# Two transformer blocks on one core: the second feed-forward switches to the normalised x one chunk earlier, and eight modulation products move to the first feed-forward

## The reference, cut to what matters

```python
mod = silu(c) @ w_mod + b_mod                    # 2048 x 12288 weights
sh1, sc1, g1, sh2, sc2, g2 = split(mod, 6)
h = rmsnorm_2(x, mlp_norm_g) * (1.0 + sc2) + sh2
u = relu(h @ w_ff1)                              # second feed-forward
x = x + g2 * ((u * u) @ w_ff2)
```

## Time and profile before

| | |
|---|---|
| median of 3 runs | 2254.77 us (2253.86 to 2256.92) |
| the profiled execution | 2253.62 us |
| its span, first to last instruction | 2251.9 us |
| granted TensorE clock, mean | 0.999 |
| PE busy | 99% of the span |
| DVE busy | 82% |
| ACT busy | 52% |

### The profile page before, as it was taken

One profiled execution on the slowest core, in us unless ns is written; L12 is line 12 of the kernel. 1 busy time (PEld: TensorE's weight loads), 2 busy tenths in 40 slices (PEclk: granted clock), 3 DMA queues, 4 the chain that ended last, 5 costly groups with the idle time before them and its releaser, 6 DMA issues.

```text
span 2251.9 us, 34334 instructions
## 1 busy us (share of the span) xinstructions
PE 2229.9 (99%) x12802; PEld 1968.5 (87%) x12802; DVE 1846.7 (82%) x2873; ACT 1167.4 (52%) x1709; POOL 111.3 (5%) x211
## 2 busy tenths in 40 slices
PE   8999999999999999999999999999999999999998
PEld 7888889888888888888899899989988888888886
DVE  7887989899889898998889888998766666666666
ACT  6554665565445454454456668556644444434444
POOL 0000000000111111111010000000000000000000
PEclk9999999999999999999999999999999999999999
DMA  8556664578888888888875554556655555555553
GB/s 318 187 180 249 234 219 157 187 248 293 307 296 305 296 298 311 297 303 300 305 267 186 200 202 150 187 202 227 227 187 187 187 189 203 187 187 194 196 190 112
DMA packets 86883, 515.61 MB, mean 229 GB/s; under 512 B 9781, under 2 KB 10341, under 8 KB 37584
## 3 DMA queue, kind: packets, MB, share of 16 engines
q1 hardware_dynamic: 57600, 406.87, 49.9%
q0 software_dynamic: 28992, 106.43, 14.2%
q10 hardware_dynamic: 144, 0.26, 0.0%
HBM read 511.39 MB, written 2.14 MB: 228 GB/s over the span
## 4 chain that ended last, share of the span: by engine, by line
PE 89%; DVE 7%; ACT 2%; issue 1%; DMA 1%; SPq 0%; ACTq 0%; POOLq 0%; DVEq 0%
PE ps L588 22%; PE ps L602 11%; PE ps L912 8%; PE ps L911 8%; PE ps L910 8%; PE ps L662 8%; PE ps L667 4%; PE ps L658 3%; PE ps L659 3%; PE ps L660 3%; DVE wl L1665 3%; PE ps L694 1%; PE ps L696 1%; PE ps L695 1%; PE ps L739 1%; DVE modraw L1773 1%
## 5 line engine op out<-in xcount | busy, mean ns | idle before, releaser
L1665 DVE TENSOR_TENSOR wl<-raw,wh 128x1024 fp32r<-128x1024 f32 x762 | 928.8, 1221 | 293.9 <-ACT wh L1109 291.1
L1109 ACT ACTIVATE wh<-raw 128x1024 fp32r<-128x1024 f32 x766 | 805.4, 1056 | 637.0 <-PE ps L912 309.1
L588 PE MATMUL ps<-xs,wh 128*128 128x512 f32 x1744 | 417.1, 390 | 0.0
L588 PEld LDWEIGHTS ps<-xs,wh 128*128 128x128 f32 x1744 | 322.6, 188 | 63.8
L1773 DVE CUSTOM_DVE_ANT_0 modraw<-modraw,cb 128x1024 f32<-128x1024 f32 x192 | 233.6, 1219 | 18.8 <-DMA modraw<-in_wmod 18.4
L602 PE MATMUL ps<-xs,wl 128*128 128x256 f32 x1744 | 227.1, 283 | 0.0
L602 PEld LDWEIGHTS ps<-xs,wl 128*128 128x128 f32 x1744 | 221.9, 191 | 5.8
L662 PE MATMUL ps<-xs,wh 128*128 128x512 f32 x880 | 223.5, 396 | 0.0
L662 PEld LDWEIGHTS ps<-xs,wh 128*128 128x128 f32 x880 | 158.3, 189 | 29.7 <-issue 0.6
L588 PE MATMUL ps<-xc,wh 128*128 128x512 f32 x608 | 150.2, 389 | 0.0
L538 POOL DMA_DIRECT2D modraw<-in_wmod x172 | 90.8, 528 | 1041.4 <-DVE modp L1773 1037.9
(11 more groups left out here) (368 smaller groups left out, 3550.4 us busy)
## 6 DMA issues: line engine op xcount, KB each, us to landing
raw<-in_w SPq DMA_DIRECT2D x381, 1024.0 KB, 5.0
modraw<-in_wmod POOLq DMA_DIRECT2D x192, 512.0 KB, 4.8
x<-in_x SPq DMA_DIRECT2D x4, 512.0 KB, 8.9
raw<-in_w SPq DMA_DIRECT2D x4, 512.0 KB, 8.8
tbias<-rel_rows POOLq DMA_DIRECT2D x4, 512.0 KB, 6.5
cb<-c_silu POOLq DMA_DIRECT2D x1, 1024.0 KB, 4.8
g2row<-g_rows POOLq DMA_DIRECT2D x1, 1024.0 KB, 10.9
finrow<-in_fin POOLq DMA_DIRECT2D x1, 1024.0 KB, 5.1
```

The lines of the kernel that those rows point to most:

```text
L588: m = nc.tensor.matmul(PS[(b + bi) % 4][:, :], hi[:, t * P:(t + 1) * P], src[k].rearrange("p a t -> p (a t)"), start=opens and first and n ...
L1109: nc.scalar.activation(wh[:, h % HS, :], raw[:, u % RAW, (h % 2) * 1024:(h % 2 + 1) * 1024], ACT.Copy).then_inc(s_round, 1)
L1665: nc.vector.tensor_tensor(wl[:, h % HS, :], raw[:, (h // 2) % RAW, (h % 2) * 1024:(h % 2 + 1) * 1024], wh[:, h % HS, :].bitcast(F32), ALU. ...
```

## The change

The second chunk of the second feed-forward now reads `xs`, in paired units, like the chunks after it. For this the 16 blocks of `h` are made in units 2 to 7 (2, 3, 3, 2, 3, 3 of them) and PE waits for them ahead of the second chunk. `normed_lo` of a block comes in the same unit as its `normed`, no longer one unit later. The second chunk's results go the way of the later chunks (`units` with `relu2` on DVE). `LATE_MODS` is 10: no modulation product is left in the second feed-forward, `g2` is made in its second unit, and in four of the five down stages of the first feed-forward DVE makes 11 products and not 9 (two each at j = 2, 4 and 6, before only at j = 4). The products between take the places of earlier ones; none is added in all.

```diff
-        normed_in = lambda u: share(KB, u, 3, 14)
-        LATE_MODS = 18
+        normed_in = lambda u: share(KB, u, 2, CH)
+        LATE_MODS = 10
...
             ups(XD, name="mlp2", late_sums=N_MLP2, joined=True, paired=False)
-            ups(XD, joined=True, paired=False)
             pe.wait_ge(s_xs, XS["mlp2n"] + KB)
+            ups(XPAIR)
...
             def relu2(n):
 
                 y, u = c.n["y"], up[:, n % 2, :]
-                if n == CH:
-                    act.wait_ge(s_modu, NMOD)
                 add_bias("ffn2", n, u, ACT.Relu)
...
-            for n in range(2 * CH):
+                h_hi(hs2[0], n)
+
+            for n in range(CH):
                 step((lambda: root(N_MLP2)) if n == 2 else (lambda: relu2(n - 1)) if n > 2 else None,
-                     late=(lambda: (relu2(0), relu2(1))) if n == 2 else lambda: hi_normed(normed_in(n)))
+                     late=lambda: (relu2(0) if n == 2 else None, relu2(1) if n == 2 else None, hi_normed(normed_in(n))))
...
+            act.wait_ge(s_modu, NMOD)
+            ups2(hs2[1], lambda: relu2(CH - 1))
...
-                token_downs(chunk, lambda: gate_in(CH - 1), lambda: conv(CH - 1), lambda j: mods(1 + (j == 4)))
+                token_downs(chunk, lambda: gate_in(CH - 1), lambda: conv(CH - 1), lambda j: mods(1 + (j in (2, 4, 6))))
...
             def second_half(n):
-                if n < CH:
-                    mods(1)
-                if n == CH:
+                if n == 1:
                     dve.wait_ge(s_modu, NMOD)
                     mod_parts(5, 6, s_g2)
                 if n >= 3:
-                    h_lo(hs2[(n - 1) // CH], (n - 1) % CH)
-                normed_lo(normed_in(n - 1))
-
-            for n in range(2 * CH):
+                    h_lo(hs2[0], n - 1)
+                normed_lo(normed_in(n))
+
+            for n in range(CH):
                 half((lambda: relu_in(n - 1)) if n > 2 else None, after=lambda: first_half(n))
                 half((lambda: (relu_in(0), relu_in(1))) if n == 2 else None, after=lambda: second_half(n))
+            units(CH, relu2, first=lambda: relu_in(CH - 1), lo_first=lambda: h_lo(hs2[0], CH - 1), h_lo_of=lambda j: h_lo(hs2[1], j))
```

More of the change, by code:

```diff
@@ L1599, in relu2 @@
                 nc.scalar.activation(yf[:, y % 2, :], u, ACT.Square).then_inc(s_hy, 1)
-                h_hi(hs2[n // CH], n % CH)
-            for n in range(2 * CH):
+                h_hi(hs2[0], n)
+            for n in range(CH):
                 step((lambda: root(N_MLP2)) if n == 2 else (lambda: relu2(n - 1)) if n > 2 else None,
-                     late=(lambda: (relu2(0), relu2(1))) if n == 2 else lambda: hi_normed(normed_in(n)))
+                     late=lambda: (relu2(0) if n == 2 else None, relu2(1) if n == 2 else None, hi_normed(normed_in(n))))
             def x_by_token(i):
@@ L1625, in final @@
                     root_table()
+            act.wait_ge(s_modu, NMOD)
+            ups2(hs2[1], lambda: relu2(CH - 1))
             for n in range(NC2 - 2):
-                downs2((lambda: h_hi(hs2[(n + 1) % 2], CH - 1)) if n else lambda: relu2(2 * CH - 1), x_by_token if n == 0 else None)
+                downs2(lambda: h_hi(hs2[(n + 1) % 2], CH - 1), x_by_token if n == 0 else None)
                 ups2(hs2[n % 2])
@@ L2527, in _ @@
             for n in range(NC2 - 2):
-                downs2(n, (lambda: relu2(CH - 1)) if n else lambda: relu_in(2 * CH - 1),
+                downs2(n, lambda: relu2(CH - 1),
                        lo_first=lambda: h_lo(hs2[(n + 1) % 2], CH - 1))
```

## The result

The changed kernel takes 2267.89 us (median of 6 runs, 2267.28 to 2275.3) against 2253.69 of the kernel before (6 runs, 2253.3 to 2256.92) beside it: ratio 1.0066, 95% interval 1.0056 to 1.0075. Predicted were 2267 us. The profiled execution took 2267.29 us with a span of 2265.6, 13.7 more than before. The sum was right, but it is not built as predicted, as the rows show.

A forecast was written before the change was run, and what follows sets the result against it. PE was taken as the bound, 89% of the chain. Own time 2253.62 + 12.8 (four downs) + 0.1 (wait for h 2.0 less 1.9 gained) = 2266.5; the median lies 1.15 above, so 2267 us, range 2256 to 2283.

The forecast's parts named there:

- Eight products more in four down stages: First feed-forward: two tile buffers delay each down's last product 6.3 us, PE waits 3.2 us a down, 12.8 in all.
- the predicted slack of 3.1: Second unit after a down: a down's last product may come 3.1 us later before PE waits for its low weights.
- The landing: Product tiles in the downs: a load lands 6.05 us after its start, giving one product per 3.97 us.
- my own criterion: Four downs: the price begins where a tile's landing exceeds 5.2 us.
- What the waits show: DVE's waits for `modraw`: 30 us or more rather than 18.4, nearly all of the rise in the four downs.
- The new wait for h: Second feed-forward, ahead of the first paired unit: PE waits 2.0 us for all 16 blocks of h.
- PE's list: Second chunk of the second feed-forward: eight paired units of 5.54 us instead of 5.78 take 1.9 us less.
- `g2` earlier, products gone: nothing: Second feed-forward: eight products and 4 MB of loads leave, `g2` is written earlier, all costed at nothing.
- The tiles come in time: Rival, four downs: landing stays at or below 5.2 us and slack takes the rest; 2253.6 to 2255, chance 0.20.
- The DMA engines fill up: Rival, downs: DMA 0.93 busy, landing 7 us or more, PE waits 7 or more a down; over 2276, chance 0.20.
- ACT and DVE fall behind in units 2 to 7: Rival, second feed-forward: at 1 us more a unit PE waits 5 us for h; 2258 if tiles come in time, chance 0.04.
- The whole saving shows: Rival: no wait at 1577 and no lost down; 2252.9, 0.08% less; faster by over 0.2% has chance 0.01.

The follow-up runs named there:

- products only: Kernel before, with only the eight modulation products moved from the second feed-forward into four down stages of the first; 2266.16 us.
- DVE's work alone: Kernel before, with two low parts of weights made a second time in each of the four downs, no load added; 2254.58 us.
- one product more: Kernel before, with ten products in each of four downs (two each at j = 2 and 6), four left in the second feed-forward; 2256.31 us.
- doubles late: Changed kernel, with the doubled products of a down behind units 5, 6 and 7 instead of 2, 4 and 6; 2282.77 us.
- spread to the gates: Changed kernel, with the eight products moved one to each down and one to each gate stage of the first feed-forward; 2264.33 us.
- ten joined: The run switch only, with h spread over ten joined units and six paired ones following; second feed-forward 93.64 us against 93.88 before.
- nine joined: The run switch only, with h spread over nine joined units and seven paired ones following; second feed-forward 94.25 us against 93.88 before.
- doubles early: Changed kernel, with the doubled products of a down behind units 0, 2 and 4 instead of 2, 4 and 6; 2265.31 us.
- switch only: Changed kernel, with the eight products taken out of the downs and made in the per-layer gate projection; 2258.18 us.
- ten joined in place: Changed kernel, with the eight products left in the second feed-forward's first chunk and ten joined units; PE waits 5.66 us, total time not given.
- switch in place: Changed kernel, with the eight products left in the second feed-forward's first chunk, switch after eight units; 10.2 us more than before.

## Why the prediction was right, point by point

**Eight products more in four down stages.** The mechanism held: products alone 11.7 us, DVE's work alone nothing, and the loss follows the position of the doubles. The place and the pace held as well (3.88 us a product against 3.97, eight starts 31.0 against 31.8). The term was 12.8 us and the stretch lost 12.2, but the agreement is partly luck. (The recorded sum, 2266.5 + 1.15, comes to 2267.7 and not to 2267.) "PE waits 3.2 us a down" is wrong in size: the waits are 1.45 us behind the first down (0.56, 0.39, 0.50), 2.30 behind the second, 0.42 and 1.92 in and behind the third, 1.06 behind the fourth (0.68, 0.15, 0.23), 7.15 in all, and not 12.8. The sum had no term for the rest: 3.4 us of lower clock, 1.1 us of matmuls counted to their end ahead of a wait, 0.8 us untraced.

The slack is what held best. In the kernel before the last product of each down starts 43.3 us after the down's first matmul. In all ten downs of these runs that themselves ran no longer than before, and whose last product came more than 3.3 us later, PE's wait in the second unit behind the down is the lateness less 3.25 us, to 0.01. With the 0.16 us by which the profile shows a wait too short, that is the predicted slack of 3.1:

```
last product later by    wait of PE    run, down
3.94, 5.56               0.68, 2.30    changed kernel, fourth and second
5.61, 5.77               2.36, 2.52    products only, fourth and third
3.55                     0.29          one product more, second
4.14, 5.46               0.89, 2.21    doubles late, second and fourth
7.84, 8.19               4.59, 4.93    doubles late, first and third
4.53                     1.27          spread to the gates, fourth
```

What was mis-sized is the lateness: 6.3 us was predicted for every down, and in the changed kernel it was 2.5, 5.6, 5.9 and 3.9. The rival that the added loads hold up the weights' own isn't what happened: in the whole stretch no engine waits for `raw`.

**The landing.** I took 6.05 us, the mean of four medians. After the change the medians of the four downs are 5.7, 5.1, 4.9 and 5.2: all but the first at or below 5.2, where my own criterion says that the price begins. Last groups of the DMA view, changed kernel, second and fourth down:

```profile
modraw<-in_wmod POOLq DMA_DIRECT2D x9, 512.0 KB, 5.1
...
modraw<-in_wmod POOLq DMA_DIRECT2D x10, 512.0 KB, 5.2
```

So the median was the wrong number to sum with: turns in sequence take their mean, and the long landings weigh in it. From the pace itself, 2 x 3.88 - 1.89 = 5.9 us; the mean of the nine landings in that down is 6.05 us, with a median of 5.1. That it equals the 6.05 taken is luck: the means of the four downs were 6.2 to 6.7 before and are 5.6 to 6.05 after, so the landings became shorter. "If `modraw` lands in 5 us there and PE doesn't wait, the prediction is wrong": it landed in 5, and PE did wait. The GB/s of the four downs are 317, 301, 299 and 315, against 310, 318, 316 and 321 before, so the engines did not fill up. By the fit of the Trainium skill (DMA: Bandwidth & Descriptors, section Anatomy of one DMA), 3.2 us for 512 KB as an estimate, nothing would have been lost; the shortest landing in these four downs is 3.5 us and their means 5.6 us and more, so the trace doesn't agree with it beside the weights' loads. The loads of `modraw` that the kernel before issues at 1445.93 and 1463.17, with no other load in flight, land in 3.54 and 3.59 us, near it.

**What the waits show.** DVE's wait for `modraw` is over 30 us, as forecast. But not nearly all of the rise is in the downs: there it goes from 11.6 to 27.0 us, and from 18.2 to 42.9 in the whole stretch between the first and the fifth down. The lateness is carried on into the up and gate stages.

**The new wait for h.** Predicted 2.0 us, measured 2.94; the mechanism is the one walked out. Where the size is off shows in the timeline of DVE, changed kernel, the last unit ahead of the wait:

```profile
1586.49 0.42 DVE L1828 TENSOR_TENSOR tb<-ps,rstd 128x258 f32<-128x258 f32 x1
1586.83 1.22 DVE L1665 TENSOR_TENSOR wl<-raw,wh 128x1024 fp32r<-128x1024 f32 x1
1587.96 1.27 DVE L1865 SCALAR_TENSOR_TENSOR yn<-x,gmod,rstd 128x256 f32<-128x256 f32 x3
1589.35 1.23 DVE L1665 TENSOR_TENSOR wl<-raw,wh 128x1024 fp32r<-128x1024 f32 x1
1590.49 0.42 DVE L2197 TENSOR_TENSOR hs2a<-yf,hs2a 128x256 fp32r<-128x256 f32 x1
1590.82 1.27 DVE L1837 SCALAR_TENSOR_TENSOR xs<-yn,mod,xs 128x256 fp32r<-128x256 f32 x3
1592.01 0.42 DVE L1828 TENSOR_TENSOR tb<-ps,rstd 128x258 f32<-128x258 f32 x1
```

A unit with three blocks is 5.52 us, not 5.33: three `normed` with what follows take 1.39 rather than 1.20 us. Some four such units make 0.8 of the 0.94 us.

**PE's list.** Predicted -1.9 us. The second chunk took 1576.96 to 1623.04 before, 46.1 us, and 44.6 after: -1.5. A joined unit is 5.76 rather than 5.78 (0.2 us in eight), a paired one 5.56 rather than 5.54 (11.11 us for two in the timeline above, 0.1 in eight), and the first high run was 0.15 slower. From start to start the wait is 3.1 us (1588.93 + 0.12 to 1592.15), so 3.1 - 1.5 = +1.6 where the sum had +0.1. The unit's rate from two starts a third of a microsecond apart was too coarse for a difference of 4%.

**`g2` earlier, products gone: nothing.** Right. The write is issued at 1555.00, which is the predicted 1543 plus the 12.1 us by which this chunk starts later, and takes 11.5 us against 11.1 before, and no wait of PE follows it until the one for h, which DVE releases. The run "products only" shows the other half.

**The rivals.** "The tiles come in time" is refuted by the products alone. "The DMA engines fill up" is not what happened (299 to 317 GB/s). "ACT and DVE fall behind in units 2 to 7" didn't happen in the changed kernel, but it is what happens where the products stay (6.26 us a unit, 5.66 and 9.09 us of wait), so the move has a reason. "The whole saving shows" would have needed no wait for h: with ten joined units it is 0.24 us.

**Left open.** Why the clock stayed at 1.00 behind the 2.94 us wait in the changed kernel and fell behind the same wait in four other kernels. How much of the landing is due to weights in flight. A third buffer for `modraw`, which would test the turn directly, was not tried. No version was found that beats the kernel before: the two nearest, nine and ten joined, can't be told from it.

## What to carry to other kernels

A wait for a double-buffered load in the middle of an in-order queue is priced by the chain of turns (reuse to issue, issue to landing) against when each item is due, not by bytes or busy time: the same eleven loads a down cost 5, 12 or 19 us in the profiled executions by where the doubles stood. Take the pace from the mean landing, not the median, and don't put the extra items late in a stage. Where a saving on the path is 0.1% of the time, measure first what its preparation adds elsewhere: here it was 12 us for a saving of 1.5.

## What the runs showed of the hardware

**A short wait of PE is followed by a lower clock.** Behind waits of 1.86 us and more the granted clock was 0.50 for some 3 us after PE had resumed, behind those of 4.59, 5.66 and 9.09 us for 4 to 5, and those matmuls ran at half speed. In some it fell before the wait's end, in others up to 1.4 us after it. The means of windows of 3 to 5 us behind each wait (the longer ones, and those that start ahead of the fall, hold full clock too):

```
wait us            clock in the window behind it
0.89               1.00   doubles late
1.36               1.00   products only
1.51, 1.51         1.00   doubles early, nine joined
1.86               0.57   spread to the gates
1.92, 2.30         0.66, 0.55   changed kernel
2.21, 4.59, 4.93   0.57, 0.50, 0.57   doubles late
2.36, 2.52         0.62, 0.65   products only
2.94               1.00   changed kernel, ahead of h
2.94, 2.94         0.66, 0.67   doubles early, spread to the gates
2.95, 2.95         0.68, 0.72   switch only, doubles late
3.57, 4.17         0.55, 0.63   one product more a down
5.66, 9.09         0.50, 0.54   ten joined in place, switch in place
```

Of these seventeen waits above 1.8 us one has no fall behind it. The 3.4 us at 0.50 behind the wait of 2.30 cost 1.7 us of work, so that wait costs 4.0 us. Two such falls are 3.4 of the 12.2 us lost in the first feed-forward.

**Successive matmuls.** 512 columns are issued every 0.227 us, 256 every 0.12 and 258 every 0.12 us, at a clock of 1.00; the lengths in the timelines (0.28, 0.39) overlap. Only differences of starts give the pace.
